# Second mixer's last products on VectorE, the output weights' second half in another slot, GpSimd's last wait removed

## What is computed

```python
def rglru_direction(uh, w_r, b_r, w_i, b_i, lam, reverse):
    ...
    r = sigmoid(einsum(uh, w_r) + b_r); i = sigmoid(einsum(uh, w_i) + b_i)
    log_a = -RG_C * r * softplus(-lam)
    a = exp(log_a)
    gated = sqrt(-expm1(2.0 * log_a)) * (i * u)
    _, h = lax.associative_scan(_linear_combine, (a, gated), axis=1, reverse=reverse)
    return h

def rglru_mixer(xn, ...):
    y_branch, u = split(xn @ w_in, 2)
    y_branch = gelu(y_branch)
    u = depthwise_conv(u, conv_w, (2, 1)) + conv_bias
    h = rglru_direction(u, forward ...) + rglru_direction(u, backward ...)
    return (y_branch * h) @ w_out
```

## Time and profile before

| what | us |
|---|---|
| median of 3 runs | 2070.02 |
| lowest and highest | 2066.43, 2072.88 |
| the profiled execution | 2071.73 |
| its span, first to last instruction | 2069.9 |
| TensorE busy | 1962.5 (95%) |
| VectorE busy | 750.5 (36%) |
| ScalarE busy | 436.3 (21%) |
| GpSimd busy | 104.3 (5%) |

### The profile page before, as it was taken

The page is one execution under the profiler, slowest core; times in us unless marked ns, Lnnn a source line. Parts: engine busy times, 40 slices in busy tenths (PEclk is TensorE's granted clock), DMA queues, the critical chain, the costliest instruction groups (busy, mean ns, idle before and its releaser), DMA issues.

```text
span 2069.9 us, 21327 instructions
## 1 busy us (share of the span) xinstructions
PE 1962.5 (95%) x8334; PEld 973.3 (47%) x8334; DVE 750.5 (36%) x1982; ACT 436.3 (21%) x886; POOL 104.3 (5%) x128
## 2 busy tenths in 40 slices
PE   7999999999999889999899999999889899999997
PEld 4444555444444335444364444444424564644554
DVE  3111354221121143455344421211115448954563
ACT  2000010111111024167010111111013422123453
POOL 0000000000000010024200000000001000000000
PEclk9999989999999999999889999999989999997999
DMA  6187179999999991110638999999997212210000
GB/s 281 41 162 292 65 303 407 428 428 428 428 427 429 424 375 64 61 62 1 264 132 340 414 428 428 428 428 428 429 415 263 87 72 81 82 41 1 15 17 11
DMA packets 46756, 512.80 MB, mean 248 GB/s; under 512 B 5296, under 2 KB 5424, under 8 KB 17328
## 3 DMA queue, kind: packets, MB, share of 16 engines
q1 hardware_dynamic: 38192, 481.38, 57.0%
q0 software_dynamic: 8448, 29.89, 3.8%
HBM read 484.90 MB, written 26.35 MB: 247 GB/s over the span
## 4 chain that ended last, share of the span: by engine, by line
PE 84%; DMA 6%; DVE 5%; issue 2%; ACT 1%; POOL 1%; SPq 0%; DVEq 0%; POOLq 0%
PE ps L947 21%; PE ps L986 9%; PE ps L488 8%; PE ps L920 7%; PE ps L585 5%; PE ps L1346 5%; PE ps L1794 5%; DMA ring<-in_wexp 4%; PE ps L1509 4%; PE ps L1984 3%; PE ps L2120 3%; PE ps L1540 3%; PE ps L2157 1%; PE ps L1011 1%; PE ps L2138 1%
## 5 line engine op out<-in xcount | busy, mean ns | idle before, releaser
L947 PE MATMUL ps<-ring,arena 128*48 128x512 f32 x1568 | 406.1, 608 | 37.0 <-issue 22.4
L947 PEld LDWEIGHTS ps<-ring,arena 128*48 128x48 f32 x1568 | 122.4, 126 | 239.4 <-issue 238.3
L960 DVE TENSOR_TENSOR arena<-arena,ps 48x512 f32<-48x512 f32 x64 | 44.1, 690 | 460.9 <-ACT arena L954 460.8
L986 PE MATMUL ps<-ring,arena 128*48 128x512 f32 x800 | 180.8, 593 | 1.1 <-ACT arena L974 1.1
L920 PEld LDWEIGHTS ps<-arena,h 128*128 128x128 f32 x1024 | 158.6, 190 | 44.6 <-issue 44.6
L920 PE MATMUL ps<-arena,h 128*128 128x192 f32 (+1 forms) x1024 | 174.3, 326 | 0.0
L947 PE MATMUL ps<-arena 128*48 128x512 f32 x480 | 159.1, 611 | 0.9 <-issue 0.9
L488 PE MATMUL ps<-arena,ring 128*128 128x512 f32 x368 | 158.1, 593 | 0.0
L954 ACT ACTIVATE arena<-ps 48x512 f32<-48x512 f32 x64 | 37.8, 590 | 474.9 <-PE ps L947 474.9
L1794 PE MATMUL ps<-ring,arena 128*128 128x512 f32 (+3 forms) x384 | 134.3, 505 | 0.0
L585 PE MATMUL ps<-ring,arena 128*128 128x512 f32 x256 | 118.2, 616 | 8.7 <-DMA ring<-in_wall 5.4
(11 more groups left out here) (284 smaller groups left out, 2128.2 us busy)
## 6 DMA issues: line engine op xcount, KB each, us to landing
ring<-in_wexp SPq DMA_DIRECT2D x148, 2048.0 KB, 19.3
arena<-in_wexp SPq DMA_DIRECT2D x44, 2048.0 KB, 21.7
ring<-in_wall SPq DMA_DIRECT2D x26, 2048.0 KB, 8.5
y_d<-arena POOLq DMA_DIRECT2D x60, 192.0 KB, 7.0
yo_d<-arena SPq DMA_DIRECT2D x2, 4032.0 KB, 41.9
xs_d<-h POOLq DMA_DIRECT2D x8, 512.0 KB, 3.6
ring<-in_wall SPq DMA_DIRECT2D x4, 1024.0 KB, 7.7
ring<-in_wall SPq DMA_DIRECT2D x2, 1536.0 KB, 6.5
```

The costliest lines, as they stand in the source:

```text
L947: mm = pe.matmul(outs[m], xeT[:, e_ // 4 % 2, k, e_ % 4 * CAP:(e_ % 4 + 1) * CAP], ws[m][:, k, :], start=(k == 0), stop=(k == KT - 1))
L986: mm = pe.matmul(outs[c], hT_of(e_ % 2)[:, k, :], w[:, k, c * 512:(c + 1) * 512], start=(k == 0), stop=(k == 3))
```

## The change

1. `plan` gets a parameter `avoid`: slots whose last unit has that key are not chosen. The two units ("out", 1, c) are planned with `avoid="b_scratch"`.
2. In the second mixer VectorE makes all eight products of `yT` and `hs`, and the last four additions of the two scans. The products 0 to 3 stand on VectorE between the two halves of the second direction; addition and product 4 to 7 stand each behind its block's scan.
3. GpSimd keeps the sixteen `gated` and the first four additions, and does them in a new order: gated for k = 0 to 11, then addition c and gated for k = 12 + c in turn.
4. GpSimd's program no longer ends with the wait for the output's stores.

```diff
@@ -154,9 +154,10 @@
         planned = []
         SLOTS = [ring[:, s * UNIT:(s + 1) * UNIT] for s in range(RING)] + [ar(15408, UNIT), ar(19504, UNIT)]
 
-        def plan(key, src, width, *freed, slots=RING):
-
-            s = min(range(slots), key=lambda q: last[q][0] if q in last else -1)
+        def plan(key, src, width, *freed, slots=RING, avoid=None):
+
+
+            s = min((q for q in range(slots) if q not in last or last[q][1].key != avoid), key=lambda q: last[q][0] if q in last else -1)
             before = last[s][1].freed if s in last else ()
             if s >= RING and key[1] == 1 and s in last and last[s][1].key[1] == 0:
                 before = before + (("b_y", 8),)
@@ -198,7 +199,7 @@
         plan(("gates", 1), W[next(wat)], UNIT, ("b_gm", 32))
         plan(("b", 3), W[next(wat)], UNIT, ("b_mm", 16))
         for c in range(2):
-            plan(("out", 1, c), W[next(wat)], UNIT, ("op_mm", 8 + 7 + c))
+            plan(("out", 1, c), W[next(wat)], UNIT, ("op_mm", 8 + 7 + c), avoid="b_scratch")
         plan_moe(1)
         GROUPS = [("qi", 320), ("kc", 284), ("qn", 512), ("qd", 512), ("ks", 384), ("v", 384)]
         for c, (g_, w_) in enumerate(GROUPS):
@@ -1604,6 +1605,11 @@
                         st.did(o)
                     else:
                         o.then_inc(S["uct"], 1)
+            def product(c):
+
+                dve.wait_ge(S["by"], c + 1)
+                dve.tensor_tensor(yT[:, c, :], yT[:, c, :], hs[:, c, :], ALU.mult).then_inc(S["b_y"], 1)
+
             for d in range(2):
                 for hf in range(2):
                     R_, I_ = bR[hf], bI[hf]
@@ -1626,36 +1632,29 @@
                         else:
                             o = dve.tensor_tensor_scan(bT[:, cc, ::-1], R_[:, cc, ::-1], I_[:, cc, ::-1], 0.0, ALU.mult, ALU.add)
                         o.then_inc(S["b_sc"], 1)
+                        if d == 1 and hf == 1:
+                            dve.wait_ge(S["b_sc"], k + 1)
+                            st.did(dve.tensor_tensor(hs[:, c, :], hs[:, c, :], bT[:, cc, :], ALU.add))
+                            st.wait()
+                            product(c)
+                    if d == 1 and hf == 0:
+                        for c in range(4):
+                            dve.wait_ge(S["b_hs"], c + 1)
+                            product(c)
 
         def pool_mixer_b(pool):
-            def gated(d, hf):
-                for cc in range(4):
-                    c = 4 * hf + cc
-                    k = 8 * d + c
-                    pool.wait_ge(S["b_gs"], 2 * k + 2)
-                    pool.tensor_tensor(bI[hf][:, cc, :], bI[hf][:, cc, :], uc[:, c, :], ALU.mult).then_inc(S["b_iu"], 1)
-
-            def both(c):
-
+            def gated(k):
+                d, c = divmod(k, 8)
+                hf, cc = divmod(c, 4)
+                pool.wait_ge(S["b_gs"], 2 * k + 2)
+                pool.tensor_tensor(bI[hf][:, cc, :], bI[hf][:, cc, :], uc[:, c, :], ALU.mult).then_inc(S["b_iu"], 1)
+
+            for k in range(12):
+                gated(k)
+            for c in range(4):
                 pool.wait_ge(S["b_sc"], 8 + c + 1)
-                pool.tensor_tensor(hs[:, c, :], hs[:, c, :], bT[:, c % 4, :], ALU.add).then_inc(S["b_hs"], 1)
-
-            def product(c):
-                pool.wait_ge(S["by"], c + 1)
-                pool.wait_ge(S["b_hs"], c + 1)
-                pool.tensor_tensor(yT[:, c, :], yT[:, c, :], hs[:, c, :], ALU.mult).then_inc(S["b_y"], 1)
-
-            gated(0, 0)
-            gated(0, 1)
-            gated(1, 0)
-            for c in range(4):
-                both(c)
-            gated(1, 1)
-            for c in range(4):
-                product(c)
-            for c in range(4, 8):
-                both(c)
-                product(c)
+                pool.tensor_tensor(hs[:, c, :], hs[:, c, :], bT[:, c, :], ALU.add).then_inc(S["b_hs"], 1)
+                gated(12 + c)
 
 
         QK = ar(4096, 17, 512)
@@ -2409,7 +2408,6 @@
                     pool_mixer_b(pool)
                     pool_rows_out(pool, 1, 4)
             pool_hgain(pool)
-            pool.wait_ge(S["out"], 16 * NT)
 
         block = ctx.enter_context(nc.Block())
```

## The result

Four runs of the changed kernel took 2046.14 us in the median (2044.83 to 2048.88), the kernel before beside them 2068.22 us (2061.11 to 2072.88). The ratio is 0.9899 with a 95% interval of 0.9877 to 0.9921: 20.9 us faster, 16 to 25 by the interval. Forecast were 2049.7 us, 20.3 less than before, with a range of 2045 to 2058.5. The profiled execution took 2048.88 us with a span of 2047.0, 22.9 less than that of before.

A forecast was written before the change was run, and what follows sets the result against it. The prediction took TensorE, busy 95% of the span, as the bound, held up in the second mixer, plus GpSimd's DRAIN at the exit. Median 2070.0 less 12.8 (mixer) and 7.5 (exit) gave 2049.7 us, range 2045 to 2058.5.

The forecast's parts named there:

- The stall for the load: Second mixer's output: TensorE's 5.43 us wait for the output weights' second half goes, with the clock lost by it.
- the load and its clock: Second mixer's output products: 9.5 us of the 12.8 us gain, from the earlier load and the clock its lateness costs.
- the earlier `b_y` 8: VectorE's last product in the second mixer comes near 992.0 instead of 995.3 us: 3.3 us of the 12.8.
- VectorE's tail: End of the second mixer: multiply, scan, addition, product take 3.34 us a column; the last product ends near 992.0 us.
- the wait for the first gelu: Second mixer: VectorE's product 4 waits for ScalarE's first gelu, near 981.2 us, and ends near 981.95.
- the gap of 0.4: Second mixer's output: TensorE has work until 991.6 us, then waits some 0.4 us for the last column.
- The interleaving on GpSimd: Second mixer: taking turns with VectorE by 1.68 and 2.17 us, GpSimd's fourth addition delays ScalarE's Tanh by 3.2 us.
- Kept to the end: After the second mixer: the whole 12.8 us arrives behind the transfer-bound experts, 1.5 us allowed either way.
- The exit: Program end: without the last wait GpSimd's DRAIN runs under the attention; gain 7.5 us, bounds 0 and 7.6.
- Rival (a): Program end: GpSimd's long DRAIN stays at the exit, so only the mixer gains; 2057.2 us, chance 0.08.
- Rival (c): Output stage: TensorE's lower clock stays, each of six products takes 13.7 instead of 6.9 us; 2091 us, chance 0.01.
- (d): Before the first expert: the slow stretch at clock 0.50, costing up to 5 us, falls elsewhere; 2045 us, chance 0.06.

The follow-up runs named there:

- e1: The kernel before with only the new slot for the output weights' second half; ratio 0.9964 to the kernel before.
- e2: The kernel before with only the products and additions on VectorE and GpSimd's new order; ratio 0.9981 to the kernel before.
- e8: The changed kernel with GpSimd's four additions ahead of its last four gate multiplies; ratio 0.9888 to the kernel before.
- e3: The kernel before without GpSimd's last wait for the output's stores, nothing else; ratio 0.9975 to the kernel before.
- e5: The kernel before with one more DRAIN on GpSimd, behind its last transfer and ahead of its last wait; timed once, 2062.40 us.
- e4: The changed kernel with GpSimd's last wait put back; ratio 0.9955 to the kernel before.
- e10: The changed kernel with GpSimd's four additions first, the same program as e8, run again; ratio 0.9897 to the kernel before, median 2050.90 us.

## Why the prediction was right

**The stall for the load.** Right in kind. In the prediction the load and its clock were 9.5 us and the earlier `b_y` 8 3.3. Alone they are 7.67 (e1) and 3.32 (e2), 10.99 together, and both at once 12.78. The 1.8 us that no part gives alone are the clock: with either gap left, TensorE is slowed behind it (9.69 us for 18 matmuls in e1, 10.08 for 16 in e2), with neither it is not. With the shortest of the four unchanged stages, 25.99 us, this share would be 3.1 us; e1 and e2 were profiled once each. The prediction's split put all of this to the load; its sum is untouched by that. Its remark that the second product took 9.84 us because the granted clock was 0.50 there holds for the first part alone: the five microseconds from 1005 had 0.67, those from 1010 had 1.00.

**VectorE's tail.** VectorE's timeline of the changed kernel:

```profile
963.42 5.63 DVE L1611 TENSOR_TENSOR arena<-arena 128x512 f32<-128x512 f32 x4
969.13 0.69 DVE L1620 TENSOR_TENSOR arena<-ring 128x512 f32<-128x512 f32 x1
...
974.84 0.69 DVE L1628 TENSOR_TENSOR ring<-ring,arena 128x512 f32<-128x512 f32 x1 [0.31 <-ACT arena L1587]
...
978.66 0.69 DVE L1611 TENSOR_TENSOR arena<-arena 128x512 f32<-128x512 f32 x1 [1.14 <-ACT arena L1591]
...
981.97 0.69 DVE L1611 TENSOR_TENSOR arena<-arena 128x512 f32<-128x512 f32 x1
...
985.28 0.69 DVE L1611 TENSOR_TENSOR arena<-arena 128x512 f32<-128x512 f32 x1
...
988.59 0.69 DVE L1611 TENSOR_TENSOR arena<-arena 128x512 f32<-128x512 f32 x1
```

The products 4 to 7 start 3.31 us apart (3.34 in the sum). The bracket at 978.66 is the wait for the first gelu that the prediction named. The last product ends at 989.28; with the 2.56 us by which this execution is ahead that is 991.84 in the clock of before, against 992.0. TensorE runs 0.38 us longer than the 13.9 us of its two products without a wait (14.28), the gap of 0.4.

**The interleaving on GpSimd.** GpSimd's and ScalarE's timelines of the changed kernel:

```profile
956.89 1.71 POOL L1656 TENSOR_TENSOR arena<-arena 128x512 f32<-128x512 f32 x1
958.56 2.18 POOL L1650 TENSOR_TENSOR ring<-ring,arena 128x512 f32<-128x512 f32 x1
960.70 1.71 POOL L1656 TENSOR_TENSOR arena<-arena 128x512 f32<-128x512 f32 x1
...
966.19 1.71 POOL L1650 TENSOR_TENSOR ring<-ring,arena 128x512 f32<-128x512 f32 x1
```

```profile
966.34 0.72 ACT L1583 ACTIVATE arena<-ring,nspt 128x512 f32<-128x512 f32 x1 [3.00 <-POOL arena L1656]
```

GpSimd and VectorE take turns at 1.67 and 2.14 us, as read from the earlier trace rows. By the whole-instruction lock of the Trainium skill (SBUF — State Buffer, "SBUF: two separate sides") with solo durations a pair would take an estimated 1.95 us or more, and that sum does not fit. The lock itself is not ruled out by it: a multiply of 0.69 us on VectorE alone lets the next one start after 0.60 (978.66 to 979.26), so a duration is not the time for which the other engine is kept out. The fourth addition holds the Tanh by 3.00 us (3.2 in the sum). All four additions and the last gating end within 0.2 us of the sum, in the clock of before. e8 shows that this delay costs 0.38 us at TensorE.

**Kept to the end.** From the third product to the first expert are 70.88 us in before (1012.95 to 1083.83) and 70.89 here (997.61 to 1068.50); from there to the exit's branch 978.1 and 978.0. The whole 12.8 us went through the transfer-bound experts, as argued. The agreement to 0.1 us is luck: over all profiled executions the first stretch took 67.1 to 70.9 us and the second 972.1 to 981.5, in both with overlap between the kernels with the old and the new mixer.

**The exit.** 7.5 forecast, 7.6 measured in the trace. Rival (a), a DRAIN that belongs to the exit, is ruled out by e3 and e5. The Trainium skill (VectorE: DVE Perf Modes, "The DRAIN you can't avoid") gives about 12 ns for the DRAINs that the runtime puts around a kernel, on all five engines. The other engines' DRAINs at the exit are near that (8 to 17 ns), GpSimd's is so (49 ns) only when another has gone before it; whether these are the DRAINs that the page means, no run here shows.

**Not forecast.** The profile's other 2.6 us, which are of the execution. The median of before was 2068.2 in the comparison and not 2070.0, so the difference (20.3 forecast, 20.9 measured) is the fairer number than the time itself. With an interval of 16 to 25 us, that the two agree to 0.6 us is luck; that the stage and the exit gained what the sum says is shown by the profiles. Rival (c) did not appear in any of the runs. (d) did not appear in the changed kernel's profile, where the slow stretch ahead of the first expert is as before; in e8's first execution it was shorter, 68.7 us from the third product to the first expert (997.32 to 1066.04) for 70.9. That is not the change either: with the old mixer e3 and e5 took 68.8.

## What to carry to other kernels

When a data wait and a transfer hang on the same semaphore value, they are paid one after the other, as here; look up which earlier-free buffer the transfer could use, and take both away together: here either gap that was left had slower matmuls behind it. Give GpSimd its exit early: whatever it waits for last stands ahead of its DRAIN. And when a step is put on a busier engine, work the chain through to the engine that bounds: here 3 us of new delay cost 0.4 us.

## What the runs showed of the hardware

GpSimd's first DRAIN behind its work took 7.59 us at the end of four profiled executions (before, e1, e2, e4), to the nanosecond the same, and 7.87 to 8.63 us in the seven where it stood right behind its last transfer; a second one took 49 ns. Gaps of 1.77 and 1.50 us with 1.13 us of matmuls between them were enough to have the next matmuls run partly at the lower of TensorE's two clock levels (e1, granted 0.66 over 5 us), while one gap of less than 0.4 us was not (1.00 from 985 to 1000 us in the changed kernel). The same program's profiled spans differed by 12.3 us (e8 and e10, 2038.6 and 2050.9, at mean granted clocks of 0.985 and 0.978).
